# A decoder layer on one core: the first quarter of the dilated heads' projection as seven products instead of eight

## The chip, the core and the metric

The kernel runs on one core of a Trainium2 chip. The metric is the time of one execution in device microseconds, taken as the median of several runs. The core has a matrix engine (PE, or TensorE; its weight loads are shown apart as PEld), a vector engine (DVE), a scalar engine (ACT), a general engine (POOL, or GpSimd), and SyncE (SP), which here only issues transfers. Each engine works through its own list of instructions in order. Semaphores hold an engine back until another has got as far as it must.

## The reference, cut to what matters

The layer has 256 tokens and a width of 2048. All is float32.

```
proj   = rms_norm(x) @ w_in                 # queries, keys, values of 8 + 8 heads, and two gates ga, gb
o_a    = forgetting attention of the 8 fox heads       (256 x 1024)
o_b    = dilated attention of the 8 dilated heads      (256 x 1024)
merged = sigmoid(ga) * (o_a @ w_br_fox) + sigmoid(gb) * (o_b @ w_br_dil)
x      = x + merged @ w_out
x      = x + causal conv-SwiGLU feed-forward of rms_norm(x)
```

The change is in `o_b @ w_br_dil`, a product of 256x1024 by 1024x2048.

## The kernel before, in words

Every large product is cut in units. A unit is one weight tile of two K tiles by 512 columns (128x1024 numbers, 512 KB). SP loads it into one of four raw buffers (`raw`). ACT copies it to a rounded high part (`w_hi`, `high(n)`, line 1480), DVE subtracts that and keeps the rest as the low part (`w_lo`, `low(n)`, line 2086), and PE multiplies three times: high by high, high by low, low by high. Both parts lie in a ring of six (`RING = 6`). So `high(n + 6)` and `low(n + 6)` follow unit n on PE (semaphore `used`), and PE starts unit n when `lo_done` has reached it.

`rows_unit` (lines 874 to 878) is the usual unit: two K tiles, both blocks of 128 tokens, three matmuls each, which makes twelve matmuls of 128x128 by 128x512. A product unit, as `gate_product` or `out_product` issue them, has one block of 128 tokens only, which may be a sum of blocks, against a weight tile that may be a sum of tiles. It has six matmuls. A 2x2 block product needs eight of them plainly and seven by Strassen's and Winograd's scheme. The gates, the output projection and the feed-forward use that scheme already.

The branch stage is 32 row units: 16 for the fox heads (c = 0 to 3 column chunks of 512, u = 0 to 3 pairs of K tiles) and then 16 for the dilated heads. The fox chunks carry the last four softmax heads (12 to 15) between their units: scores after u = 0 (`attend_scores`), transposes of the probabilities after u = 3 (`attend_transpose`), the product with the values after the next chunk's first unit (`last_values`). After each chunk DVE multiplies the two banks by the gates (`fox_part`, `dil_part`). After each dilated chunk it adds both branches into `tmp`, and PE transposes the sum by eight small matmuls (`transpose_block`, line 925) after u = 2 of the next chunk; ACT and DVE split it for the output projection (`merged_high`, `merged_low`).

What sets the order is written out by hand: each engine's loop goes over the units and has its extra work at named units. SP issues branch loads four ahead: load m waits for `lo_done` of load m - 4, which used the same raw buffer. Between them, at m = 14, 17, 20 and 23 (`PAIR_LOADS_AT`), it issues the first four loads of the output projection's own seven-product pair, into `raw_y` and `raw_x`. POOL prepares the bias of softmax heads 13, 14 and 15 (`prepare_dil`, lines 2788 and 2790), each after the row maximum of the head before, and then issues the adding transfers of the output pair (`third_sum`, `first_sum`, line 2814). An adding transfer reads a tile from HBM and adds it to what lies in SBUF; it goes through POOL's software queue.

Of the kernel before, what the change touches and what calls it, by code (L numbers as in the profile page):

```python
# [6 lines left out]
P = 128  # L7
SEQ = 256
# [101 lines left out]
OUT_UNIT = BR_UNIT + 4 * UPR  # L110
# [22 lines left out]
FF_UNIT = OUT_UNIT + len(OUTS)  # L133
GATE_PARTS = ("P3", "P5", "P6")


def raw_use(n):

    if n < GATE_UNIT:
        return n % RAW_SLOTS, n // RAW_SLOTS + 1  # L140
    if n < BR_UNIT:
        k = GATE_LOAD_AT[GATES[n - GATE_UNIT]]
    elif n < OUT_UNIT:
        k = n - BR_UNIT + len(GATE_LOADS)
    else:
        k = OUT_LOAD_AT[OUTS[n - OUT_UNIT]] + 4 * UPR + len(GATE_LOADS)
    return k % RAW_SLOTS, (GATE_UNIT + k) // RAW_SLOTS + 1

# [41 lines left out]
def br_banks(m):  # L190
    return (0, 2) if m % 2 else (1, 3)
# [7 lines left out]
PAIR_LOADS_AT = {14: (1, 0), 17: (1, 1), 20: (0, 0), 23: (0, 1)}  # L199
# [9 lines left out]
TAIL_MADE = {"P5": 13, "P6": 14, "P7": 15, "P3": 16}  # L209
# [60 lines left out]
FIRST_SLOTS = (8, 9, 0, 1, 2, 3)  # L270
# [29 lines left out]
def load_count(k):  # L300

    before = raw_use(FF_UNIT - 1)[1] if slot_of(k) < RAW_SLOTS else 0
    return before + sum(slot_of(m) == slot_of(k) for m in range(k + 1))
# [34 lines left out]
def decoder_layer(nc, x, x_t, smalls, consts, w_in, w_fox, w_dil, w_out, w_up, w_down, decay_dram, out):  # L338
# [15 lines left out]
    with ctx:  # L354
# [116 lines left out]

        def last_of(name, k):
# [70 lines left out]
        def last_sum(m):  # L543
# [25 lines left out]
        xt_in = [sem(f"xt_in{u}") for u in range(UPR)]  # L569
        smalls_in, consts_in, wf_in, x_again, out_done = (  # L570
            sem("smalls_in"), sem("consts_in"), sem("wf_in"), sem("x_again"), sem("out_done"))
        second_tile, third_tile = sem("second_tile"), sem("third_tile")
        first_tile, gains_in, tile_high, tile_split, warm_data = (
            sem("first_tile"), sem("gains_in"), sem("tile_high"), sem("tile_split"), sem("warm_data"))
# [38 lines left out]
        d_seeded = sem("d_seeded")  # L613
        row_max, den_ready, rden_ready, dil_merged, tap1, ss_ready, fa_sum, fa_neg = (
            sem("row_max"), sem("den_ready"), sem("rden_ready"), sem("dil_merged"), sem("tap1"),
            sem("ss_ready"), sem("fa_sum"), sem("fa_neg"))
        decay_rows = [sem(f"decay_rows{m}") for m in range(4)]
# [8 lines left out]
        def _(sp):  # L626
# [11 lines left out]
            def load_late(n, src):  # L638

                if n >= BR_UNIT + RAW_SLOTS:  # L640
                    sp.wait_ge(lo_done, n - RAW_SLOTS)
                s = raw_use(n)[0]
                sp.dma_start(raw[:, s, :].rearrange("p (k n) -> p k n", k=KU), src).then_inc(w_loaded[s], 16)

            def br_tile(m):
                c, u = m // 4 % 4, m % 4
                return (w_fox_v if m < 16 else w_dil_v)[:, KU * u:KU * u + KU, NB * c:NB * c + NB]
# [91 lines left out]
            for n, unit in enumerate(GATES, GATE_UNIT):  # L739
                if unit[0] != "H":  # L740
                    k = GATE_LOAD_AT[unit] + RAW_SLOTS
                    sp.wait_ge(lo_done, n)
                    if k < len(GATE_LOADS):
                        load_gate(k)
                    else:
                        m = k - len(GATE_LOADS)
                        load_late(BR_UNIT + m, br_tile(m))
                    continue
# [10 lines left out]
            for m in range(RAW_SLOTS, 4 * UPR):  # L759
                load_late(BR_UNIT + m, br_tile(m))  # L760
                if m in PAIR_LOADS_AT:
                    side, q = PAIR_LOADS_AT[m]
                    if side:
                        sp.wait_ge(lo_done, GATE_AT["H", PAIRS - 1, "P4", q])
                        load_gate_b22(PAIRS, q)
                    else:
                        sp.wait_ge(y_added[q], 2 * PAIRS)
                        load_gate_b11(PAIRS, q)
# [95 lines left out]
        def _(pe):  # L864
# [273 lines left out]
            def branch_unit(m, u):  # L1138
                pair = [bank[b] for b in br_banks(m)]
                kt = KU * u if m < 4 else KT // 2 + KU * u  # L1140
                rows_unit(BR_UNIT + 4 * m + u, actB, (kt, kt + 1), pair, u == 0, u == 3)
# [23 lines left out]
            for c in range(4):  # L1165
                if c < 2:
                    pe.wait_ge(fox_merged, 3 + c)
                else:
                    pe.wait_ge(dil_merged, c - 1)
                for u in range(4):  # L1170
                    if c == 0 and u == 1:
                        pe.wait_ge(kept_lo, 1)
                    elif c == 0 and u > 1:
                        pe.wait_ge(o_lo, 12 + 2 * (u - 1))
                    branch_unit(4 + c, u)
                    if c == 0 and u == 0:
                        last_values(3)
                    if c and u == 2:
                        pe.wait_ge(merged, c)
                        transpose_block(lambda r, col: tmp[:, r, col:col + P], bank[4:6], mt_ready)  # L1180
# [7 lines left out]
            def out_product(n, name, q):  # L1188

                if q == 0:  # L1190
                    if name == "P3":
                        pe.wait_ge(dil_merged, 3)
                        pe.wait_ge(h_part_lo, 5)
                    elif name == "P1":
                        pe.wait_ge(dil_merged, 4)
                        pe.wait_ge(h_part_hi, 9)
                    elif name == "P7":
                        pe.wait_ge(h_part_lo, 6)
                    elif name == "P6":
                        pe.wait_ge(h_part_lo, 7)  # L1200
                        pe.wait_ge(g_p1, PAIRS + 1)
                    elif name == "P5":
                        pe.wait_ge(h_part_lo, 8)
# [36 lines left out]
            for n, unit in enumerate(OUTS, OUT_UNIT):  # L1240
# [6 lines left out]
                else:  # L1247
                    u = unit[1]
                    if u == 0:
                        pe.wait_ge(g_c22, PAIRS)  # L1250
# [98 lines left out]
            def tail_product(n, name):  # L1349
# [11 lines left out]
                if name in TAIL_PARTS:  # L1361
                    pe.wait_ge(h_part_lo, 8 + TAIL_PARTS.index(name) + 1)
# [60 lines left out]
        def _(act):  # L1423
            def high(n):
# [3 lines left out]
                if pair_product(n):  # L1428
# [14 lines left out]
                    else:  # L1443
                        act.wait_ge(y_added[q], 2 * c + 2)
                elif n < FF_UNIT:
# [328 lines left out]

            for c in range(4):
                for u in range(4):
                    high(BR_UNIT + 4 * c + u + RING)
# [7 lines left out]
                    elif u == 3:  # L1785
                        copy_pt(12 + c)

            for c in range(4):
                for u in range(4):
                    high(BR_UNIT + 16 + 4 * c + u + RING)  # L1790
                    if c == 0 and u == 0:
                        out_high(15)
                    elif c and u == 2:
                        merged_high(c - 1)
                    elif c == 3 and u == 1:
                        act.wait_ge(mt_lo, 2)
                        merged_part_high("P3", 12)
                        for half in range(2):
                            nc.scalar.activation(own[:, 0, :, half * P:half * P + P],
                                                 gate_quarter(0, 0, half).bitcast(f32), ACT.Copy, scale=-1.0)\  # L1800
                                .then_inc(h_part_hi, 1)
# [14 lines left out]
            for n, unit in enumerate(OUTS, OUT_UNIT):  # L1816
# [9 lines left out]
                if unit == ("C", 0):  # L1826
                    merged_part_high("P7", 12)
                elif unit == ("H", PAIRS, "P3", 0):
                    merged_part_high("P6", 12)
                elif unit == ("H", PAIRS, "P3", 1):  # L1830
                    merged_part_high("P5", 12)
# [235 lines left out]
        def _(dve):  # L2067
            def low(n):
# [4 lines left out]
                if pair:  # L2073
                    _, c, name, q = pair
                    src = raw_x[:, q, :] if name in ("P1", "P5", "P2") else raw_y[:, q, :]
                elif n < FF_UNIT:
# [340 lines left out]
            def fox_part(c):  # L2417
                dve.wait_ge(used, BR_UNIT + 4 * c + 4)
# [6 lines left out]
            def dil_part(c):  # L2425
                dve.wait_ge(used, BR_UNIT + 16 + 4 * c + 4)
                for r in range(RT):
                    part = gb[:, r, c * NB:(c + 1) * NB]
                    t = nc.vector.tensor_tensor(part, bank[br_banks(4 + c)[r]], part, ALU.mult)
                t.then_inc(dil_merged, 1)  # L2430
# [3 lines left out]
                                        ALU.add).then_inc(merged, 1)  # L2434

            for c in range(4):
                for u in range(4):
# [5 lines left out]
                    low(BR_UNIT + 4 * c + u + RING)  # L2443
                    if u == 0:
# [3 lines left out]
                        softmax_head(12 + c, prep, True)  # L2448

            def make_merged():  # L2450
# [3 lines left out]
                dve.wait_ge(h_made, 9)  # L2454
                nc.vector.tensor_tensor(x21, x11, x21, ALU.subtract).then_inc(h_made, 1)
                dve.wait_ge(h_made, 10)
                nc.vector.tensor_tensor(x11, x11, x22, ALU.subtract).then_inc(h_made, 1)
                dve.wait_ge(h_made, 11)
# [8 lines left out]
            for c in range(4):  # L2467
                for u in range(4):
                    if u == 3:
                        if c:  # L2470
                            merged_low(c - 1)
                            dve.wait_ge(mt_ready, 2 * c)
                        dil_part(c)
                    low(BR_UNIT + 16 + 4 * c + u + RING)
                    if c == 0 and u == 0:
                        out_low(15)
                    elif c == 3 and u == 0:
                        make_merged()
                    elif c == 3 and u == 2:
                        merged_part_low("P3", 7)  # L2480
# [42 lines left out]
            for n, unit in enumerate(OUTS, OUT_UNIT):  # L2523
# [7 lines left out]
                if unit == ("C", 0):  # L2531
                    merged_part_low("P7", 10)
                elif unit == ("H", PAIRS, "P3", 1):
                    merged_part_low("P6", 11)
                elif unit == ("C", 1):
                    merged_part_low("P5", 12)
# [105 lines left out]
            def tail_low(name):  # L2642

                dve.wait_ge(h_part_hi, 12 + TAIL_PARTS.index(name) + 1)
# [130 lines left out]
        def _(pool):  # L2775
            def prepare_fox(h):
# [3 lines left out]
                pool.wait_ge(decay_rows[h // 2], 32)  # L2780
# [68 lines left out]
            for c in range(1, 4):  # L2849
                prepare_dil(12 + c).then_inc(prep_ready, 1)  # L2850
# [90 lines left out]
```

## Time and profile before

| what | us |
|---|---|
| median of 3 runs | 1331.04 |
| lowest and highest | 1330.64, 1331.25 |
| the profiled execution's own time | 1331.1 |
| its span, first to last instruction | 1329.3 |
| PE busy | 1324.8 |
| DVE busy | 1147.9 |
| ACT busy | 959.9 |
| POOL busy | 167.1 |

The granted TensorE clock was 1.000 over the whole span. The chain of work that ended last lies on PE for 100% of the span. The profile's matmul durations overlap, since matmuls are pipelined: the distance between two starts says more than the duration of one.

### The profile page before, as it was taken

The numbers are of one execution on the slowest core, as the hardware profiler recorded it, in microseconds if no ns is written. First come the engines' busy times: TensorE is split into PE (matmuls) and PEld (weight loads), VectorE is DVE, ScalarE is ACT, GpSimd is POOL, SyncE is SP. The second block draws the span as 40 slices with busy tenths as digits, with TensorE's granted clock in tenths as the row PEclk, the third lists the DMA queues.
The fourth block names the chain that finished last, engine by engine and source line by source line (L and its number), as shares of the span: only waits on it lengthen the run. The fifth ranks groups of instructions, "written<-read, shape, count | busy, mean of one in ns | idle before, by whom it ended". The sixth has DMA issues, their size and how long they took to land.

```text
span 1329.3 us, 16539 instructions
## 1 busy us (share of the span) xinstructions
PE 1324.8 (100%) x6037; PEld 1098.8 (83%) x6037; DVE 1147.9 (86%) x1369; ACT 959.9 (72%) x1214; POOL 167.1 (13%) x186
## 2 busy tenths in 40 slices
PE   9999999999999999999999999999999999999999
PEld 7888888888888888888888888888888888888887
DVE  6868887888878876888689898999999999999998
ACT  6666666566666654567777878888888888888874
POOL 0121212021011000101010101111111102020201
DMA  9877685758888665488879798999989899999996
GB/s 355 290 170 262 142 259 119 244 156 229 230 218 226 219 207 205 129 238 260 288 174 332 161 303 172 314 220 282 248 252 267 230 281 222 294 213 315 192 294 176
DMA packets 120720, 312.03 MB, mean 235 GB/s; under 512 B 12088, under 2 KB 13376, under 8 KB 120384
## 3 DMA queue, kind: packets, MB, share of 16 engines
q1 hardware_dynamic: 92192, 235.10, 50.9%
q0 software_dynamic: 23824, 71.84, 30.4%
q10 hardware_dynamic: 4624, 4.05, 1.0%
q8 instruction: 48, 0.79, 0.2%
q14 instruction: 32, 0.26, 0.1%
HBM read 308.84 MB, written 2.11 MB: 234 GB/s over the span
## 4 chain that ended last, share of the span: by engine, by line
PE 100%; DVE 0%; POOL 0%; issue 0%; POOLq 0%
PE acc L874 12%; PE acc L878 12%; PE acc L876 12%; PE acc L912 9%; PE acc L916 9%; PE acc L914 9%; PE acc L1103 4%; PE acc L1099 4%; PE acc L1101 4%; PE acc L1076 3%; PE acc L1078 3%; PE acc L1074 3%; PE acc L1266 1%; PE acc L897 1%; PE acc L893 1%; PE acc L895 1%
## 5 line engine op out<-in xcount | busy, mean ns | idle before, releaser
L2086 DVE TENSOR_TENSOR w_lo<-raw,w_hi 128x1024 fp32r<-128x1024 f32 x225 | 272.7, 1219 | 67.1 <-ACT w_hi L1480 65.7
L1480 ACT ACTIVATE w_hi<-raw 128x1024 fp32r<-128x1024 f32 x225 | 235.1, 1054 | 86.7 <-PE acc L878 50.2
L874 PE MATMUL acc<-w_hi,actA 128*128 128x512 f32 x580 | 228.3, 394 | 0.0
L878 PE MATMUL acc<-w_hi,actA 128*128 128x512 f32 x580 | 226.1, 390 | 0.0
L876 PE MATMUL acc<-w_lo,actA 128*128 128x512 f32 x580 | 225.8, 389 | 0.0
L1480 ACT ACTIVATE w_hi<-raw_y 128x1024 fp32r<-128x1024 f32 x152 | 158.1, 1058 | 72.9 <-PE acc L878 21.9
L2086 DVE TENSOR_TENSOR w_lo<-raw_y,w_hi 128x1024 fp32r<-128x1024 f32 x152 | 182.8, 1219 | 18.4 <-ACT w_hi L1480 16.8
L2086 DVE TENSOR_TENSOR w_lo<-raw_x,w_hi 128x1024 fp32r<-128x1024 f32 x116 | 139.8, 1220 | 45.4 <-ACT w_hi L1480 45.2
L1480 ACT ACTIVATE w_hi<-raw_x 128x1024 fp32r<-128x1024 f32 x116 | 119.8, 1052 | 47.9 <-DMA raw_x<-w_in 23.0
L878 PEld LDWEIGHTS acc<-w_hi,actA 128*128 128x128 f32 x580 | 108.9, 188 | 22.9
L874 PEld LDWEIGHTS acc<-w_hi,actA 128*128 128x128 f32 x580 | 108.9, 188 | 21.9 <-issue 0.2
L876 PEld LDWEIGHTS acc<-w_lo,actA 128*128 128x128 f32 x580 | 109.0, 188 | 21.8
L912 PE MATMUL acc<-w_hi,actB 128*128 128x512 f32 x296 | 116.3, 393 | 0.0
L916 PE MATMUL acc<-w_hi,actB 128*128 128x512 f32 x296 | 115.4, 390 | 0.0
L914 PE MATMUL acc<-w_lo,actB 128*128 128x512 f32 x296 | 115.1, 389 | 0.0
L1099 PE MATMUL acc<-w_hi,actA 128*128 128x512 f32 x224 | 88.3, 394 | 0.0
L1103 PE MATMUL acc<-w_hi,actA 128*128 128x512 f32 x224 | 87.3, 390 | 0.0
L1101 PE MATMUL acc<-w_lo,actA 128*128 128x512 f32 x224 | 87.2, 389 | 0.0
L1480 ACT ACTIVATE w_hi<-odd 128x1024 fp32r<-128x1024 f32 x64 | 67.5, 1054 | 19.6 <-PE acc L916 9.9
L2086 DVE TENSOR_TENSOR w_lo<-odd,w_hi 128x1024 fp32r<-128x1024 f32 x64 | 77.9, 1217 | 1.8 <-ACT w_hi L1480 1.8
L2857 POOL DMA_DIRECT2D raw_y<-w_up x34 | 29.5, 867 | 376.2 <-DVE w_lo L2086 376.0
L2561 DVE SCALAR_TENSOR_TENSOR work<-acc,smalls_sb,work 128x255 f32<-128x255 f32 (+1 forms) x176 | 72.4, 472 | 3.2 <-ACT work L1863 3.1
(385 smaller groups left out, 2779.5 us busy)
## 6 DMA issues: line engine op xcount, KB each, us to landing
raw<-w_in SPq DMA_DIRECT2D x101, 512.0 KB, 4.8
raw<-w_down SPq DMA_DIRECT2D x59, 512.0 KB, 5.6
raw_x<-w_up SPq DMA_DIRECT2D x44, 512.0 KB, 5.0
raw_y<-w_up POOLq DMA_DIRECT2D x34, 512.0 KB, 7.6
raw_x<-w_in SPq DMA_DIRECT2D x28, 512.0 KB, 4.2
odd<-w_up SPq DMA_DIRECT2D x27, 512.0 KB, 5.1
work<-w_up SPq DMA_DIRECT2D x24, 512.0 KB, 5.5
work<-w_up POOLq DMA_DIRECT2D x24, 512.0 KB, 8.1
```

Of the source, the lines that this page charges most:

```text
L874: nc.tensor.matmul(o, lhsT=a_h, rhs=w_hi[:, s, k, :], start=first and k == 0, stop=False, skip_group_check=onto_seed)
L876: nc.tensor.matmul(o, lhsT=a_h, rhs=w_lo[:, s, k, :], start=False, stop=False, skip_group_check=onto_seed)
L878: mm = nc.tensor.matmul(o, lhsT=a_l, rhs=w_hi[:, s, k, :], start=False, stop=last and k == KU - 1, skip_group_check=onto_seed)
L912: nc.tensor.matmul(o, lhsT=a_h, rhs=w_hi[:, s, k, :], start=first and k == 0, stop=False, skip_group_check=True)
L914: nc.tensor.matmul(o, lhsT=a_h, rhs=w_lo[:, s, k, :], start=False, stop=False, skip_group_check=True)
L916: mm = nc.tensor.matmul(o, lhsT=a_l, rhs=w_hi[:, s, k, :], start=False, stop=last and k == KU - 1, skip_group_check=True)
L1099: nc.tensor.matmul(o, lhsT=a_h, rhs=w_hi[:, s, k, :], start=side == 0 and j == 0 and k == 0, stop=False, skip_group_check=True)
L1101: nc.tensor.matmul(o, lhsT=a_h, rhs=w_lo[:, s, k, :], start=False, stop=False, skip_group_check=True)
L1103: mm = nc.tensor.matmul(o, lhsT=a_l, rhs=w_hi[:, s, k, :], start=False, stop=kt == KT - 1, skip_group_check=True)
L1480: nc.scalar.activation(w_hi[:, n % RING, :, :], src.rearrange("p (k n) -> p k n", k=KU), ACT.Copy).then_inc(hi_done, 1)
L2086: nc.vector.tensor_tensor(w_lo[:, n % RING, :, :], src.rearrange("p (k n) -> p k n", k=KU), w_hi[:, n % RING, :, :].bitcast(f32), ALU.subt ...
L2561: t = nc.vector.scalar_tensor_tensor(out=conv[:, j, lag:SEQ], in0=bank[(4, 7)[j // 2]][:, (j % 2) * SEQ:(j % 2 + 1) * SEQ - lag], scalar=s ...
```

## The change

The dilated chunks 0 and 1 over the first two pairs of K tiles (heads 8 to 11) become one 2x2 block product: two blocks of 128 tokens by two K pairs, times two K pairs by two column chunks. Its eight half units, which were four row units, become seven product units in the order P1, P7, P6, P2, P5, P4, P3. The other twelve units of the dilated heads stay row units; units (0,2), (0,3), (1,2), (1,3) now add onto banks that the products have filled.

- Four blocks of activations are summed: DVE makes four whole blocks (`dil_whole`) and four differences (`make_dil`), ACT rounds them (`dil_high`), DVE takes the low parts (`dil_low`). This is done inside the fox chunks.
- Four of the seven weight tiles are sums. Their first tiles are loaded by SP into `raw_x` and `raw_y` after branch loads 4, 5, 6 and 7 (`load_dil_base`), and POOL adds the others by seven adding transfers (`add_dil_tile`): three for P4, two for P6, one each for P7 and P5. The other three products load one tile each in the ordinary way.
- ACT copies the bank after P1, P7, P6 and P5 (`dil_copy`): P1 negated from bank 1 to bank 3, P5 from bank 1 to bank 0, P7 and P6 into the softmax buffer. PE's P6, P5, P4 and P3 wait for one of these copies each.
- DVE adds the saved P6 to chunk 0's second block, and takes the saved P7 from chunk 1's second block, ahead of the gating.
- The merged chunk 0 is transposed after unit (1,3), and was after (1,2). The merged chunk 1 is added by DVE after unit (2,0).
- The output pair's first loads move to m = 22, 23, 24 and 26 of 31.
- Four semaphores are shared with start-up ones, and counts are shifted. One load fewer in the raw ring turns the first slots of the feed-forward.

```diff
+DIL_STEPS = ("P1", "P7", "P6", "P2", "P5", "P4", "P3")
+DIL_BANKS = {"P1": 1, "P6": 1, "P5": 1, "P7": 7, "P4": 7, "P2": 3, "P3": 0}
+DIL_TILE = {"P1": (0, 0), "P2": (0, 1), "P3": (1, 1)}
+DIL_SUMS = {"P4": (0, ((1, 1), (1, 0), (0, 0), (0, 1))), "P6": (1, ((1, 1), (1, 0), (0, 0))),
+            "P7": (2, ((1, 1), (1, 0))), "P5": (3, ((0, 0), (1, 0)))}
...
-PAIR_LOADS_AT = {14: (1, 0), 17: (1, 1), 20: (0, 0), 23: (0, 1)}
+PAIR_LOADS_AT = {22: (1, 0), 23: (1, 1), 24: (0, 0), 26: (0, 1)}
+DIL_BASE_AT = {4: "P4", 5: "P6", 6: "P7", 7: "P5"}
...
+            def load_dil_base(name):
+                at, tiles = DIL_SUMS[name]
+                q = QU - 1 if name in ("P4", "P6") else 0
+                if name in ("P6", "P7"):
+                    sp.wait_ge(lo_done, GATE_AT["H", PAIRS - 1, "P4", q])
+                else:
+                    sp.wait_ge(y_added[q], 2 * PAIRS)
+                sp.dma_start(dil_at[at].rearrange("p (k n) -> p k n", k=KU), dil_tile(*tiles[0]))\
+                    .then_inc(dil_loaded[name], 16)
...
+            def dil_product(name):
+                if name == "P1":
+                    pe.wait_ge(fox_merged, 3)
+                    pe.wait_ge(h_part_hi, 8)
+                elif name == "P7":
+                    pe.wait_ge(g_c22, PAIRS)
+                elif name == "P6":
+                    pe.wait_ge(dil_out, DIL_OUT["P1"])
+                elif name == "P2":
+                    pe.wait_ge(kept_lo, 1)
+                elif name == "P5":
+                    pe.wait_ge(dil_out, DIL_OUT["P6"])
+                elif name == "P4":
+                    pe.wait_ge(dil_out, DIL_OUT["P7"])
+                elif name == "P3":
+                    pe.wait_ge(dil_out, DIL_OUT["P5"])
...
+            for unit in BRANCH[16:]:
+                if unit[0] == "Q":
+                    dil_product(unit[1])
+                    if unit[1] == "P7":
+                        last_values(3)
+                    continue
...
+            for unit in BRANCH[16:]:            # ACT
+                n = BR_AT[unit]
+                if unit == ("Q", "P7"):
+                    out_high(15)
+                if unit[0] == "Q" and unit[1] in ("P1", "P7", "P6", "P5"):
+                    dil_copy(n, unit[1])
+                high(n + RING)
...
+            add_dil_tile("P4", 1)
+            add_dil_tile("P6", 1)
+            prepare_dil(13).then_inc(prep_ready, 1)
+            add_dil_tile("P7", 1)
+            add_dil_tile("P5", 1)
+            add_dil_tile("P4", 2)
+            prepare_dil(14).then_inc(prep_ready, 1)
+            add_dil_tile("P6", 2)
+            add_dil_tile("P4", 3)
+            prepare_dil(15).then_inc(prep_ready, 1)
```

## Rows read from the trace of the kernel before

**Rows 1.** The page: PE's busy time, and DMA busy tenths in 40 slices.
```profile
PE 1324.8 (100%) x6037; PEld 1098.8 (83%) x6037; DVE 1147.9 (86%) x1369; ACT 959.9 (72%) x1214; POOL 167.1 (13%) x186
...
DMA  9877685758888665488879798999989899999996
```
**Rows 2.** Waits of PE, whole span: waiter, released by, us, times, longest.
```profile
PE acc L999 <- POOL actB L2802: 1.3, 1, 1.3
```
**Rows 3.** The chain that ended last: start, us, what.
```profile
505.79 0.33 PE acc L952 x3
...
525.88 0.87 PE acc L925 x8
537.66 0.87 PE acc L925 x8
```
**Rows 4.** Timeline of PE around the last fox unit and the first dilated one.
```profile
502.91 0.39 PE L874 MATMUL acc<-w_hi,actB 128*128 128x512 f32 x1
...
505.63 0.49 PE L952 MATMUL acc<-smalls_sb,softmax 128*128 128x128 f32 x3
505.88 0.48 PE L874 MATMUL acc<-w_hi,actB 128*128 128x512 f32 x1
...
508.71 0.59 PE L959 MATMUL acc<-softmax,odd 128*128 128x256 f32 x2
...
509.28 0.47 PE L874 MATMUL acc<-w_hi,actB 128*128 128x512 f32 x1
```
**Rows 5.** Timeline of PE in product units of the output projection.
```profile
570.15 0.39 PE L1212 MATMUL acc<-w_hi,actB 128*128 128x512 f32 x1
...
571.51 0.39 PE L1212 MATMUL acc<-w_hi,actB 128*128 128x512 f32 x1
```
**Rows 6.** Timeline of ACT in the branch stage: start, us, instruction, idle before.
```profile
505.89 1.06 ACT L1480 ACTIVATE w_hi<-raw 128x1024 fp32r<-128x1024 f32 x1 [1.66 <-PE acc L878]
506.86 0.47 ACT L1492 ACTIVATE softmax<-acc 128x384 f32<-128x384 f32 x1
...
509.94 0.37 ACT L1500 ACTIVATE actB<-acc 128x256 fp32r<-128x256 f32 x1
...
527.42 0.59 ACT L1509 ACTIVATE actA<-acc 128x512 fp32r<-128x512 f32 x1
```
**Rows 7.** ACT's groups by form, 453 to 610 us: busy us, mean ns.
```profile
L1808 ACT ACTIVATE acc<-acc 128x512 f32<-128x512 f32 x1 | 0.6, 579 | 0.0
```
**Rows 8.** Timeline of DVE: a softmax's end, a gating, and the turn between dilated chunks.
```profile
502.26 0.55 DVE L2125 TENSOR_SCALAR softmax<-softmax,st 128x128 f32<-128x128 f32 x2
...
505.83 1.29 DVE L2422 TENSOR_TENSOR work<-acc,work 128x512 f32<-128x512 f32 x2 [0.35 <-PE acc L878]
...
538.84 1.23 DVE L2086 TENSOR_TENSOR w_lo<-raw,w_hi 128x1024 fp32r<-128x1024 f32 x1 [1.50 <-ACT w_hi L1480]
539.99 1.49 DVE L2137 TENSOR_TENSOR actA<-acc,actA 128x512 fp32r<-128x512 f32 x2
...
542.73 1.23 DVE L2433 TENSOR_TENSOR tmp<-work 128x1024 f32<-128x1024 f32 x1
```
**Rows 9.** The page's DMA queues: packets, MB, share of 16 engines' span.
```profile
q1 hardware_dynamic: 92192, 235.10, 50.9%
q0 software_dynamic: 23824, 71.84, 30.4%
```
**Rows 10.** Engines and DMA share from 449 to 488 us.
```profile
449.00:488.00 39.00, 39.00 (x181) 32.48 (x180) 28.43 (x50) 23.79 (x33) 2.35 (x6) 1.00 0.68 232
```
**Rows 11.** Landing times of raw_x transfers, 380 to 600 us.
```profile
DMA to landing us min/median/max: 3.7/5.4/10.7
```
**Rows 12.** The page's DMA issues: KB, median us to landing.
```profile
raw<-w_in SPq DMA_DIRECT2D x101, 512.0 KB, 4.8
...
raw_y<-w_up POOLq DMA_DIRECT2D x34, 512.0 KB, 7.6
```
**Rows 13.** Timeline of POOL: the preparations for heads 14 and 15.
```profile
475.52 0.18 POOL L2788 COPY st<-smalls_sb 128x1 f32<-128x1 f32 x1 [11.71 <-DVE st L2105]
...
487.58 0.18 POOL L2788 COPY st<-smalls_sb 128x1 f32<-128x1 f32 x1 [10.97 <-DVE st L2105]
```

More of the change, by code:

```diff
@@ L133 @@
 FF_UNIT = OUT_UNIT + len(OUTS)
+OUT_AT_LOADS = [OUT_AT[unit] for unit in OUT_LOADS]
 GATE_PARTS = ("P3", "P5", "P6")
@@ L269 @@
 LOAD_AT = {unit: m for m, unit in enumerate(LOADS)}
[L270 removed]
+FIRST_SLOTS = (8, 9, 3, 0, 1, 2)
 SLOTS = 10
@@ L1786, in _ @@
                         copy_pt(12 + c)
[L1788 to L1801, printed above, removed]
+                    if (c, u) == (1, 1):
+                        act.wait_ge(kept_lo, 1)
+                        dil_high("P1")
+                    elif (c, u) == (2, 1):
+                        for name in DIL_PARTS[:2]:
+                            dil_high(name)
+                    elif (c, u) == (2, 2):
+                        for name in DIL_PARTS[2:]:
+                            dil_high(name)
+            for unit in BRANCH[16:]:
[5 more added lines that the diff above has]
+                high(n + RING)
+                if unit == ("L", 1, 3):
+                    merged_high(0)
+                elif unit in (("L", 2, 2), ("L", 3, 2)):
+                    merged_high(unit[1] - 1)
+                elif unit == ("L", 3, 1):
+                    act.wait_ge(mt_lo, 2)
+                    merged_part_high("P3", 20)
+                    for half in range(2):
+                        nc.scalar.activation(own[:, 0, :, half * P:half * P + P],
+                                             gate_quarter(0, 0, half).bitcast(f32), ACT.Copy, scale=-1.0)\
+                            .then_inc(h_part_hi, 1)
             def out_sum(n, name):
@@ L2465, in merged_part_low @@
                     .then_inc(h_part_lo, 1)
[L2467 to L2480, printed above, removed]
+            for unit in BRANCH[16:]:
+                if unit in (("L", 2, 3), ("L", 3, 3)):
+                    c = unit[1]
+                    merged_low(c - 1)
+                    dve.wait_ge(mt_ready, 2 * c)
+                    dil_gate(c)
+                    merge(c)
+                elif unit == ("L", 0, 3):
+                    dil_gate(0)
+                    merge(0)
+                elif unit == ("L", 1, 3):
+                    dil_gate(1)
+                low(BR_AT[unit] + RING)
+                if unit == ("Q", "P7"):
+                    out_low(15)
+                elif unit == ("L", 2, 0):
+                    merged_low(0)
+                    dve.wait_ge(mt_ready, 2)
+                    merge(1)
+                elif unit == ("L", 3, 0):
+                    make_merged()
+                elif unit == ("L", 3, 2):
+                    merged_part_low("P3", 13)
             def add_x2(n, c, banks):
```

267 lines of the change are left out of this document (201 added, 66 removed).

## The prediction, made before the changed kernel was run

> **What bounds the kernel now.** I read the page's busy times first. PE is busy for 1324.8 us of a span of 1329.3 us; DVE has 1147.9 and ACT 959.9 [rows 1]. That alone doesn't prove a bound, because matmul ends are modelled. So I read PE's waits next: over the whole span there is one, of 1.3 us, before the first matmul [rows 2]. The chain of waits then shows what the branch stage is made of. In it the chain never leaves PE, and two dilated chunks end 11.78 us apart (525.88 to 537.66) [rows 3]. The timeline shows what those 11.78 us are: one row unit of twelve matmuls takes 505.63 - 502.91 = 2.72 us, or 0.227 us per matmul [rows 4], so 48 matmuls take 10.9 us and the eight transposes 0.87. Nothing is left over. In this stage a matmul that goes is worth 0.227 us, and an edit on any other engine is worth nothing until PE has to wait for it.
>
> **What PE loses.** Four row units (48 matmuls) become seven products of six (42). A product unit's pace is not shown in this stage, but the output projection has them: six matmuls from 570.15 to 571.51 take 1.36 us [rows 5], again 0.227 each, so a product costs no start-up of its own. Saved: 6 x 0.227 = 1.36 us. The transposes, the values product and the 0.31 us start behind each of them (505.88 to the next start) stay, in the same number. The Trainium skill, "VectorE: DVE Perf Modes", section "The TRN2 errata", gives a matmul of 512 columns as 518 cycles of 2.4 GHz, 216 ns; by it the sum would be 1.30 us. The rows say 227, and the rest does without it.
>
> **The four new waits of PE on ACT.** I lay the new order over the old clock, from PE's 505.63. Transposes to 505.88; P1 to 507.33 (0.09 us slow start, as the old unit has: 508.71 - 505.88 = 2.83 for twelve); P7 to 508.69; values to 509.28 (0.57 us, 508.71 to 509.28) [rows 4]; P6 to 510.7, P2 to 512.1, P5 to 513.45, P4 to 514.8, P3 to 516.2. ACT starts its part 0.10 us behind PE's last issue (505.89 against the transposes' 505.63, of which 0.16 is the matmul's end) and hands on after 0.97 us for a `high` and 0.5 for a copy of a bank, whose full length is 0.58 to 0.59 [rows 6, 7].
> - P1's copy runs at about 507.6 to 508.2; P6 wants it at 509.28. Free by 1.1 us.
> - Then `high` to 508.9, head 15's output (0.37) after the values, about 509.5 to 509.9, P7's copy to 510.4, a `high` to 511.3, P6's copy to 511.9. P5 wants it at 512.1. Free by 0.2 us only: this is the tightest step, and what is behind it is two more `high`s, which have the ring's lead.
> - P5's copy: two `high`s, then 513.8 to 514.35; P3 wants it at 514.8. Free by 0.4 us. P4's wait for P7's copy is long over.
> A semaphore's way from ACT to PE isn't in a row; the way from PE to ACT is 0.1 to 0.26 us. The bounds of this item are 0 (all three fit) and, at most, three waits of one `high` each, 3 x 0.97 = 2.9 us, if each copy comes one `high` later. I take 0.1 us, since my clock has every copy in time.
>
> **DVE.** It gains three `low`s (3 x 1.22), two bank sums (about 0.65 each, half of 1.29 [rows 8]), eight block sums and four low parts of 128x256, for which I take 0.35 each from half a 128x512 one: 3.7 + 1.3 + 4.2 = 9.2 us over some 110 us in which it has at least 20 us idle. ACT gains three `high`s, four copies and five small roundings, about 7.5 us, and has more room. What matters is place. The block sums sit behind the softmax of their chunk, not before it: a head is finished at 502.8, and PE wants it at 505.63 [rows 4, 8], a slack of 2.8 us that no added DVE work eats. In the seven products DVE must deliver one `low` per 1.36 us of PE; it needs 1.22 plus head 15's low part, but ACT's copies throttle it to about one per 1.3 us. It enters with six units in hand and the first unit behind the products (index 23) is low at about 512.7, wanted at 516.2. Nothing there.
> The transposes of chunk 0 wait for three DVE operations and an addition (0.68 + 2 x 0.6 + 1.22 = 3.1 us), with two units (5.4 us) before them: free. Those of chunk 1 now wait for work moved behind unit (2,0). With T at the last issue of (1,3): transposes and (2,0) to T + 3.6, `high` to T + 4.8, `low` 1.15, low parts of the merged chunk 1.41 (539.99 after 538.84, as now [rows 8]), addition 1.22, in all T + 8.6. PE arrives at T + 0.87 + 2.83 + 2 x 2.72 = T + 9.1. Free by 0.5 us. If that cover goes, each us late is a us of PE. I take 0.
>
> **DMA.** Before, the four units needed four plain transfers. Now it is three plain, four bases and seven adding ones: three plain more and seven adding more. A tile is 0.524 MB, so the page's queues hold 448 plain and 137 adding ones, at 0.509 x 1329.3 / 448 = 1.51 us and 0.304 x 1329.3 / 137 = 2.95 us of all sixteen engines each [rows 9]. Added: 3 x 1.51 + 7 x 2.95 = 25 us. The stretch into which nearly all falls, 449 to 488, is now 68% busy, which is 12.5 us of room in 39 [rows 10]; two output loads leave it. So it fills up and the rest runs on to about 500. The Trainium skill, "DMA: Bandwidth & Descriptors", section "Issuing engines are not separate DMA queues", says that transfers issued by SP and by POOL run on the same 16 engines and interleave. It speaks against this change, and is the mechanism of the first rival; the trace fits it in so far as slices with 9 tenths busy exist all through the feed-forward while PE stays full [rows 1].
> What a late tile costs: a load is issued when its buffer's last user is low, about 2.4 us into an iteration, and is wanted four iterations later: 4 x 2.77 - 2.4 = 8.7 us. Landing takes 4.8 now [rows 12], 10.7 at worst near here [rows 11]. Beyond 8.7 the `high` waits and with it, in ACT's queue, the exponentials of a head; that has 2.8 us of slack, so PE waits from a landing of about 11.5 us. At the other units the ring has 11 us more. The sums themselves have time: bases from about 450, landed by 461; adding ones 7.6 us each [rows 12], of which the last two of P6 and P4 stand in POOL's queue behind head 14's preparation at 475.5 [rows 13], so done at 485 to 487. P6's tile is wanted near 496, P4's at 505.9. POOL's preparations have waited 11 us idle for DVE, so the adds ahead of them (about 1.2 us each to issue) delay none. The item is bounded by 0 and 12 us (four heads, each 3 us late); I take 0, as the nearest row, a 10.7 us maximum, is below the point.
> The moved output loads are issued near 510 to 520 and wanted after 535. Free.
>
> **The sum.** -1.36 + 0.1 = -1.3 us on the profiled execution's 1331.1 us (span 1329.3 and 1.8 around it), so 1329.8. The median shown is 1331.04, 0.06 lower: 1329.8 again. That is 0.10%. About 0.2%, or 2.7 us, is what a measurement of this kernel can tell from no change, so this is "within".
>
> **Rivals.**
> - Late tiles. The stretch from 450 to 500 asks for 22 plain and 7 adding transfers, 34 + 21 = 55 us in 50. If fox tiles behind a base and beside an adding transfer land at 14 us and not at 9, three heads come 2.5 us late each: 7.5 - 1.4 = 6 us slower, 1337. It decides from 11.5 us of landing. For it: the arithmetic above. Against it: the adds are spread in three groups, and the feed-forward lives with 90% busy. 8%.
> - ACT's copies come one `high` late in the seven products: 1 to 3 waits of 0.97 us take the place of the gain, or the 0.5 us before chunk 1's transposes turns negative: 1330.3 to 1332.5. For it: 0.2 us of slack. Against it: every duration is from a row of the same operation. 15%.
> - The change sets something free that the rows don't show, a pace below 0.227 or a shorter end: over 2.7 us faster, 1328 or below. No row speaks for it; PE had no wait to lose. 4%.
> - My forecast, 1329.3 to 1330.3: 73%.
>
> **How the numbers follow.** Faster by over 0.2% is the third rival: 0.04. Slower by over 0.2% is the first: 0.08. The rest, 0.88, is within. The range goes from 1329.2, the full 1.36 and the runs' own spread, up to 1331.7, which takes in most of the second rival, a wait of two `high`s.
>
> **What would show it.** PE from the last fox transposes to the start of unit (0,2): 10.3 us, with products 1.36 apart. A wait of PE on ACT's copy would stand before P5 first, then P3. The transposes (x8) come once after (1,3) and the merged stage ends 1.4 us earlier, and that distance is kept to the last instruction. DMA busy near 0.9 to 1 from 450 to 490, with fox landings up to 9 us. PE waiting for softmax (line 952) or for `lo_done` would prove the first rival. A gain or a loss of over 2.7 us would make the prediction wrong.

## The result: 13 us slower, and the profile after

The changed kernel took 1344.26 us (median of 5 runs, 1341.78 to 1346.02), the kernel before 1331.04 (5 runs, 1330.64 to 1331.43). The ratio is 1.0097, with a 95% interval from 1.0082 to 1.0112. I had forecast 1329.8, within 0.2%. The profiled execution took 1344.27 us, and its span is 1342.5, against 1329.3.

The page of the changed kernel, as [rows 1] before. PE's busy time is up by only 2.7 us, so 10.5 of the 13.2 us by which the span grew are idle time. A row for the clock has appeared, which means that the clock is no longer full everywhere; the mean is 0.996.

```profile
PE 1327.5 (99%) x6031; PEld 1100.1 (82%) x6031; DVE 1156.4 (86%) x1386; ACT 967.4 (72%) x1227; POOL 175.8 (13%) x193
...
PEclk9999999999999989999999999999999999999999
DMA  9877685758888795568869788999999999999996
```

The waits of PE over the whole span, as [rows 2]: two new ones. One is for the copy of head 12's probabilities, the other for the sum of the merged chunk 0.

```profile
PE acc L1024 <- ACT softmax L1608: 6.7, 1, 6.7
PE acc L990 <- DVE tmp L2603: 3.6, 1, 3.6
PE acc L1064 <- POOL actB L3017: 1.3, 1, 1.3
```

The chain that ended last, 440 to 620 us, shows what is behind each (start, us, what). Read it upward from PE. Head 12's values (line 1024) wait for ACT's copy (line 1608). ACT was there late because the `high` ahead of it waited for a fox tile that took 15.0 us from its issue to its landing. That tile was asked for late in turn, since its buffer came free only when a tile that had landed in 8.4 us was split. The second wait is further down: the merged transposes (line 990) wait for DVE's addition (line 2603), and that stands behind the split of a w_dil tile which landed in 10.1 us.

```profile
450.71 8.39 DMA raw<-w_fox
459.12 1.07 ACT w_hi L1596
460.21 1.24 DVE w_lo L2242
461.47 14.98 DMA raw<-w_fox
476.50 0.94 issue
477.44 0.48 ACT softmax L1608
477.96 1.22 PE acc L1024 x2
...
489.45 0.33 PE acc L1017 x3
...
514.67 0.33 PE acc L1017 x3
...
524.14 10.14 DMA raw<-w_dil
534.31 1.07 ACT w_hi L1596
535.44 1.11 issue
536.54 0.68 DVE softmax L2588
...
538.46 1.24 DVE tmp L2603
539.74 1.97 PE acc L990 x8
...
550.54 0.87 PE acc L990 x8
```

The `high` before that one had waited too, for the tile issued at 457.78, which landed only 16.5 us later. So had the last tile alone been in time, the copy could have come at the end of this `high`, 475.4, and not at 477.44: about 2 us of the wait hang on the last tile alone (an estimate from these starts), and the rest on both.

```profile
474.35 1.06 ACT L1596 ACTIVATE w_hi<-raw 128x1024 fp32r<-128x1024 f32 x1 [1.23 <-DMA raw<-w_fox]
```

POOL's issuing of the adding transfers was not what was late. Its preparation of head 13, which stands behind two of them, had waited 3.3 us for DVE:

```profile
465.32 0.18 POOL L3003 COPY st<-smalls_sb 128x1 f32<-128x1 f32 x1 [3.34 <-DVE st L2261]
```

The transfers' share and PE's clock in the stretches around it (us from and to, sum; busy time of PE, PEld, DVE, ACT, POOL; granted clock, DMA share, GB/s), as [rows 10]. Sixteen engines are fully used from 455 to 477. The granted clock shows 0.71 towards the end of PE's 6.7 us of idleness and 0.77 in the stretch behind it, so it stood at 1.2 GHz in part of each and at 2.4 in the rest. From 537 to 547, with the 3.6 us wait in it, it shows 0.83. From 507 to 517 the transfers are nearly idle, and from 527 they are full again.

```profile
449.00:455.00 6.00, 6.00 (x28) 4.97 (x27) 3.96 (x5) 2.55 (x3) 0.00 (x0) 1.00 0.90 292
455.00:461.00 6.00, 6.00 (x29) 5.01 (x28) 3.19 (x4) 2.69 (x3) 1.42 (x2) 1.00 1.00 351
...
473.00:477.00 4.00, 0.00 (x0) 0.00 (x0) 1.56 (x3) 1.71 (x3) 0.78 (x1) 0.71 1.09 298
477.00:487.00 10.00, 9.04 (x34) 7.54 (x35) 6.87 (x18) 6.01 (x13) 2.57 (x4) 0.77 0.99 268
...
507.00:517.00 10.00, 10.00 (x47) 8.25 (x46) 8.73 (x20) 5.01 (x10) 0.00 (x0) 1.00 0.15 52
...
527.00:537.00 10.00, 9.13 (x41) 7.22 (x39) 4.05 (x4) 3.91 (x4) 0.00 (x0) 1.00 1.00 374
537.00:547.00 10.00, 7.26 (x30) 6.25 (x31) 8.56 (x11) 5.24 (x7) 0.00 (x0) 0.83 0.57 179
```

Landing times (from issue to arrival) of the tiles issued from 449 to 480 us: the fox tiles went to 11.1 us in the median, from 4.5 in the kernel before. Over 440 to 540 us the raw tiles' landing times were 3.5, 7.1 and 16.5 us (least, median, most), and in the kernel before 3.5, 4.5 and 6.0.

```profile
raw<-w_fox SPq DMA_DIRECT2D x10, 512.0 KB, 11.1
raw_x<-w_dil POOLq DMA_DIRECT2D x3, 512.0 KB, 9.8
```

The seven products themselves (timeline of PE): from the first product's start to the first row unit behind them, 525.09 - 514.75 = 10.34 us, with no wait.

```profile
514.75 0.48 PE L1240 MATMUL acc<-w_hi,wf 128*128 128x512 f32 x1
...
525.09 0.39 PE L939 MATMUL acc<-w_hi,actB 128*128 128x512 f32 x1
```

**Where the 13 us are.** The same points of PE's program are compared with [rows 3, 4].

| stretch | before | after | difference |
|---|---|---|---|
| up to the fourth fox transposes (x3) | 505.79 | 514.67 | +8.88 |
| from there to the second merged transposes (x8) | 31.87 | 35.87 | +4.00 |
| the rest of the span | 791.6 | 792.0 | +0.3 |

Of the 8.88, 6.7 are waiting and 2.0 slow clock: from head 12's values to the next transposes (x3) it is 489.45 - 477.96 = 11.5 us, and in the kernel before it was 480.58 - 471.06 = 9.5. The 4.00 are the gain of 1.3, the wait of 3.6, and 1.7 of slow clock: the next transposes come 10.80 us later, and 9.10 in a version without the wait (e5 below).

### The profile page after: what moved, and what is told of

It reads as the page before. It is cut to its first block, busy times and chain, and to the rows that moved or that the text cites. A ratio compares the mean times of both kernels' runs of the same rounds, so it can differ in the third digit from the quotient of the medians.

```text
span 1342.5 us, 16579 instructions
## 1 busy us (share of the span) xinstructions
PE 1327.5 (99%) x6031; PEld 1100.1 (82%) x6031; DVE 1156.4 (86%) x1386; ACT 967.4 (72%) x1227; POOL 175.8 (13%) x193
## 4 chain that ended last, share of the span: by engine, by line
PE 96%; DMA 2%; DVE 1%; ACT 0%; issue 0%; POOL 0%; ACTq 0%; POOLq 0%
PE acc L939 11%; PE acc L943 11%; PE acc L941 11%; PE acc L977 9%; PE acc L981 9%; PE acc L979 9%; PE acc L1168 4%; PE acc L1164 4%; PE acc L1166 4%; PE acc L1143 3%; PE acc L1141 3%; PE acc L1139 3%; DMA raw<-w_fox 2%; PE acc L1378 1%; PE acc L958 1%; PE acc L962 1%
## 5 line engine op out<-in xcount | busy, mean ns | idle before, releaser
L1596 ACT ACTIVATE w_hi<-odd 128x1024 fp32r<-128x1024 f32 x64 | 67.4, 1053 | 19.4 <-PE acc L981 10.1
```

Source lines behind the costliest of these rows:

```text
L1596: nc.scalar.activation(w_hi[:, n % RING, :, :], src.rearrange("p (k n) -> p k n", k=KU), ACT.Copy).then_inc(hi_done, 1)
```

## The experiments

Theory A: the adding transfers and bases crowd the fox tiles, a late tile stands in ACT's queue before work that PE needs, and that is the first wait. Theory A2: the output tiles among the w_dil tiles behind the seven products are the second. The rival B: the added work on ACT, DVE and POOL, and its order, is what is late. Rival C: the bases alone, ahead of the fox tiles in SP's queue.

**e1, without the adding transfers.** The seven `add_dil_tile` calls are out, and ACT waits for the base alone.

```diff
-                    act.wait_ge(dil_summed[summed_product(n)], 16 * (len(tiles) - 1))
+                    act.wait_ge(dil_loaded[summed_product(n)], 32)
...
-            add_dil_tile("P4", 1)
-            add_dil_tile("P6", 1)
...
```

> The changed kernel without its seven adding transfers; the four base tiles are still loaded, so four weight tiles are not the sums they should be. Theory A (late tiles: the adding transfers make the fox tiles land late, ACT's queue stands behind them and PE waits 6.7 us for head 12's probabilities): the first wait and its slow clock go, 9 us; the second wait (3.6 us before the transposes of chunk 0, with 1.5 us of slow clock) has another cause and stays: 1335. Rival B (the added ACT and DVE work, or POOL's order, is late): nothing changes, 1344. Rival C (the four bases ahead of the fox tiles in SP's queue do it): nothing changes in the first wait either, 1343 to 1344.

Measured: 1335.58 us against 1331.06, ratio 1.0035 (1.0023 to 1.0047). Its waits:

```profile
PE acc L990 <- DVE tmp L2603: 2.4, 1, 2.4
PE acc L1064 <- POOL actB L3017: 1.3, 1, 1.3
PE acc L1038 <- DVE w_lo L2383: 0.2, 1, 0.2
```

The first wait is gone and the second stays, shorter. The bases alone bring the fox tiles to 6.0 us of landing, which is harmless (against C). All ACT and DVE work was kept (against B). Behind the wait of 2.4 us the eight transposes took 1.39 us and not 0.87, and the next ones came 10.91 us later, against 9.10 in e5: 1.8 us of slow clock, with the granted clock at 0.83 from 527 to 537.

**e2, the old kernel with the new traffic.** It computes as before; the bases and adding transfers are issued at the changed kernel's places, and nothing reads them. Its output loads move to the matching late places, and each waits until the sum in its buffer is complete.

```diff
+DIL_BASE_AT = {4: "P4", 5: "P6", 6: "P7", 7: "P5"}
-PAIR_LOADS_AT = {14: (1, 0), 17: (1, 1), 20: (0, 0), 23: (0, 1)}
+PAIR_LOADS_AT = {23: (1, 0), 24: (1, 1), 25: (0, 0), 27: (0, 1)}
...
+                if m in DIL_BASE_AT:
+                    load_dil_base(DIL_BASE_AT[m])
...
+            add_dil_tile("P4", 1)
+            add_dil_tile("P6", 1)
             prepare_dil(13).then_inc(prep_ready, 1)
...
```

> The kernel before, computing as before, with the changed kernel's four bases and seven adding transfers into raw_x and raw_y at the same places of SP's and POOL's orders (nothing reads the sums), and the output pair's first loads moved to the same late places (m = 23, 24, 25 and 27 of 32). Theory A: the first wait appears in the old kernel, PE waits 6 to 7 us for head 12's values, and with the slow clock it is 9 us slower: 1340. The second wait needs the burst behind the seven products and doesn't appear, or is under 1 us. Rival B: no wait of PE, 1331.

Measured: 1341.14 us, ratio 1.0070 (1.0053 to 1.0087). Its longest wait, and from its chain the transfer at the root of it:

```profile
PE acc L980 <- ACT softmax L1513: 6.9, 1, 6.9
```

```profile
461.54 15.49 DMA raw<-w_fox
```

The old kernel gets the same wait from the traffic alone, and no wait before its merged transposes. This is the cleanest proof of theory A: 10.1 us of loss without any product, copy or block sum. By the trace 9.6 of them are there at the fourth fox transposes (515.42 for 505.79) and 0.5 is lost in the output projection. (I expected 9; another wait, of 0.8 us, is of PE for a head's probabilities themselves, line 973 on DVE.)

**e3, the output pair's loads split.**

```diff
-PAIR_LOADS_AT = {22: (1, 0), 23: (1, 1), 24: (0, 0), 26: (0, 1)}
+PAIR_LOADS_AT = {20: (1, 0), 21: (1, 1), 28: (0, 0), 29: (0, 1)}
```

> The changed kernel with the output pair's first loads at m = 20 and 21 (into raw_y, free once P7 and P6 are split, where the transfers stand nearly idle from 507 to 517 us) and m = 28 and 29 (into raw_x), not at 22, 23, 24 and 26. Theory A2 (these four tiles among five w_dil tiles issued within 8 us make a w_dil tile land in 10 us, and chunk 0's gating stands behind its low part): the second wait goes and its slow clock, 5 us: 1339, the first wait untouched. Rival (the second wait is that of the three w_dil tiles that are issued late because the products free no raw buffer; the output loads don't matter): 1343 to 1344.

Measured: 1338.98 us, ratio 1.0056 (1.0041 to 1.0071), 5.3 us less than the changed kernel. The 6.7 us wait is as it was, and that for line 2603 is gone. Theory A2 holds, and its rival, the late w_dil loads alone, does not: the same five loads are issued from 519.6 to 526.1 us here, and PE doesn't wait. The w_dil tiles issued from 517 to 530 us landed in 5.7 us in the median, for 8.2.

**e4, the bases before the fox tiles and the adds spread.**

```diff
+                elif name == "P2":
+                    load_dil_base(("P5", "P4")[q])
+                elif name == "P4":
+                    load_dil_base(("P7", "P6")[q])
...
             add_dil_tile("P4", 1)
-            add_dil_tile("P6", 1)
             prepare_dil(13).then_inc(prep_ready, 1)
-            add_dil_tile("P7", 1)
-            add_dil_tile("P5", 1)
-            add_dil_tile("P4", 2)
+            add_dil_tile("P6", 1)
             prepare_dil(14).then_inc(prep_ready, 1)
+            add_dil_tile("P7", 1)
+            add_dil_tile("P4", 2)
             add_dil_tile("P6", 2)
+            add_dil_tile("P5", 1)
             add_dil_tile("P4", 3)
```

> The changed kernel with the four bases loaded at the end of the gate stage (where the transfers are 30% busy from 440 to 449 us) and the adding transfers spread: P4's first before head 13's preparation, P6's first before head 14's, the other five between head 14's and head 15's. Output pair loads untouched. Theory A in the form that it is the crowding of 455 to 477 us: the first wait falls from 6.7 to below 1 us, 1336 with the second wait as it was. Rival (too many bytes for the stage, wherever they are): PE waits 3 us or more at another fox chunk, 1340 or above.

Measured: 1338.24 us, ratio 1.0048 (1.0033 to 1.0063). This was a partial miss. The first wait went, but the four bases, now straight in front of the first fox tiles, opened one of 1.9 us inside the first fox chunk. The profile names no releaser for it ("issue"), but ACT had just stood idle for 5.9 us until a fox tile landed, its `high` starting at 455.36 us; that the bases made this tile late is likely and not shown apart. The second wait is the changed kernel's 3.6.

```profile
PE acc L992 <- DVE tmp L2605: 3.6, 1, 3.6
PE acc L941 <- issue: 1.9, 1, 1.9
```

**e5, the compute side alone.** No bases, no adding transfers, the output loads as in e3.

```diff
-                if m in DIL_BASE_AT:
-                    load_dil_base(DIL_BASE_AT[m])
...
-                    act.wait_ge(dil_summed[summed_product(n)], 16 * (len(tiles) - 1))
```

> The changed kernel without the four bases and the seven adding transfers (four weight tiles are then whatever the buffers hold, so the products are not the right ones), and with the output pair's loads split as in e3. All of the seven products, copies, block sums and waits stay. Theory A (transfers are the whole loss, and the compute side of the change works as forecast): both waits are gone, 1331.05 - 1.36 = 1329.7, between 1329.4 and 1330.3. Rival (the copies and the order of ACT and DVE cost something too, hidden so far behind the transfers): 1331 or above.

Measured: 1330.39 us against 1331.13, ratio 0.9995 (0.9986 to 1.0003); 0.1 us beyond the upper end of what I expected, and a gain that this comparison can't tell from none, so the trace has to. Chain:

```profile
505.88 0.33 PE acc L1015 x3
...
527.33 0.90 PE acc L988 x8
536.43 0.87 PE acc L988 x8
```

From the fourth fox transposes to the second merged ones it is 30.55 us, against 31.87 in [rows 3]: 1.32 us gained, where I had forecast 1.36 less 0.1. About 0.5 is lost again by 600 us, where the output projection's transposes come 0.7 earlier than before; this version, like e3 and e7, loads two of its output tiles at m = 28 and 29. The rival expected 1331 or above, and is refuted only as far as the trace goes.

**e7, all seven adds, but later.** Bases untouched, output loads as in e3.

```diff
+            prepare_dil(13).then_inc(prep_ready, 1)
             add_dil_tile("P4", 1)
             add_dil_tile("P6", 1)
-            prepare_dil(13).then_inc(prep_ready, 1)
+            prepare_dil(14).then_inc(prep_ready, 1)
             add_dil_tile("P7", 1)
-            add_dil_tile("P5", 1)
             add_dil_tile("P4", 2)
-            prepare_dil(14).then_inc(prep_ready, 1)
             add_dil_tile("P6", 2)
+            prepare_dil(15).then_inc(prep_ready, 1)
+            add_dil_tile("P5", 1)
             add_dil_tile("P4", 3)
-            prepare_dil(15).then_inc(prep_ready, 1)
```

> The changed kernel with its bases where they are (m = 4 to 7), the output pair's loads as in e3, and the seven adding transfers later: two behind head 13's preparation, three behind head 14's, two behind head 15's. Theory A with the crowding of 455 to 477 us as the cause: the wait of 6.7 us goes; if the stage has room for the adds behind it, 1330 to 1331. Theory A with too many bytes for the stage: the stretch from 475 to 505 us is full (5 adds, 15 us, with the fox and dilated tiles in 30 us) and PE waits 1 to 5 us for a later head or for P4's or P5's tile: 1332 to 1336.

Measured: 1332.20 us against 1331.13, ratio 1.0007 (0.9998 to 1.0016). The wait of 6.7 us is 1.4 now:

```profile
PE acc L1024 <- ACT softmax L1608: 1.4, 1, 1.4
```

So 12 of the 13 us come back with the same bytes, only the order changed. Two orders changed, though: e3 has the same output loads and is 7.9 us above its kernel before, e7 1.1, so 6.8 of the 12 are the adds' and the rest the output loads'. What differs in the first 28 us is not the transfers' share, but the number of adds in it, two for five, and the fox tiles' landing, 7.1 us in the median for 11.1. The stretch behind takes the other adds, 93% busy, and PE doesn't wait in it. Where the adds stand moves these late tiles; by how much each single add does was not tried. Windows of e7:

```profile
449.00:477.00 28.00, 26.62 (x122) 21.90 (x121) 19.47 (x33) 17.48 (x21) 3.39 (x4) 1.00 1.00 313
477.00:507.00 30.00, 30.00 (x142) 24.94 (x142) 24.85 (x57) 16.32 (x33) 7.99 (x9) 1.00 0.93 238
```

**e9, the bases later as well** (m = 8, 9, 10 and 12; output loads at 20, 21, 25 and 26).

```diff
-DIL_BASE_AT = {4: "P4", 5: "P6", 6: "P7", 7: "P5"}
+DIL_BASE_AT = {8: "P4", 9: "P6", 10: "P7", 12: "P5"}
```

> As e7 (all seven adding transfers), with the bases at m = 8, 9, 10 and 12 instead of 4 to 7 and the output pair's raw_x loads at m = 25 and 26 instead of 28 and 29. The 1.4 us wait of e7, which the bases among the first fox tiles cause, goes, and 0.5 us in the output projection: 1330.3 (1329.8 to 1331). Rival (the bases then crowd the adds of 475 to 500 us and a later head is late): 1332 to 1334.

Measured: 1331.06 us against 1331.28, ratio 1.0000 (0.9991 to 1.0009). Better than e7 in the median, but both theories were half right. PE is busy for all of 449 to 477, so e7's wait for the first head is gone; two shorter ones have come behind it, in a stretch that is now 98% busy; that this is their cause is argued, not shown. A third, of 0.8 us, lies in the output projection. The execution profiled here was the slowest of the eleven, 1332.56 us. The waits of PE and that window:

```profile
PE acc L1064 <- POOL actB L3017: 1.3, 1, 1.3
PE acc L1024 <- ACT softmax L1608: 0.9, 2, 0.7
PE acc L1344 <- ACT odd L1966: 0.8, 1, 0.8
```

```profile
477.00:507.00 30.00, 29.06 (x135) 23.59 (x134) 23.84 (x55) 15.73 (x30) 7.35 (x8) 1.00 0.98 270
```

**e6, fewer transfers.** P6's tile is P7's plus P1's, and P4's is P6's plus P2's. DVE makes both additions from tiles that lie in SBUF anyway. The buffers and semaphores that change with it are left out of this cut.

```diff
+                if unit in (("Q", "P7"), ("Q", "P2")):
+                    other = BR_AT["Q", "P1"] if unit[1] == "P7" else n
+                    dve.wait_ge(lo_done, n)
+                    nc.vector.tensor_tensor(dil_at[0], dil_at[0], raw[:, raw_use(other)[0], :],
+                                            ALU.add).then_inc(dil_added, 1)
...
+DIL_BASE_AT = {7: "P7", 10: "P5"}
+PAIR_LOADS_AT = {14: ((1, 1),), 20: ((0, 1),), 21: ((0, 0), (1, 0))}
...
+            prepare_dil(13).then_inc(prep_ready, 1)
+            add_dil_tile("P7", 1)
+            prepare_dil(14).then_inc(prep_ready, 1)
+            add_dil_tile("P5", 1)
+            prepare_dil(15).then_inc(prep_ready, 1)
```

> Seven products with the sums made otherwise: two bases and two adding transfers (P7's and P5's tiles); P6's and P4's tiles come from P7's by two DVE additions of 128x1024 (1.22 us each) of the tiles that P1 and P2 load anyway. Bases at m = 7 and 10, the adds behind the preparations of heads 13 and 14. The two raw_x and raw_y buffers that are now free take output tiles at m = 14 and 20, the other two at m = 21. Added against the kernel before: 1 plain and 2 adding transfers, 1.5 + 2 x 2.95 = 7 us of the transfers' time in place of 25. Theory A: no fox tile lands beyond 9 us, no wait of PE: 1329.7 (1329.4 to 1330.5). Rival (any adding transfer beside the fox stage makes tiles late): PE waits 2 us or more for a softmax head or a gating, 1332 or above.

Measured: 1331.21 us against 1331.13, ratio 1.0000 (0.9991 to 1.0010). One of the eleven executions took 2724.7 us, for which I have no cause; the others lay between 1329.96 and 1331.93. A miss: no fox tile was late (7.0 us at most), but the merged transposes waited.

```profile
PE acc L1068 <- POOL actB L3030: 1.3, 1, 1.3
PE acc L994 <- DVE tmp L2616: 0.8, 1, 0.8
PE acc L1039 <- ACT actA L1708: 0.4, 1, 0.4
```

**e8, e6 with two output loads later.**

```diff
-PAIR_LOADS_AT = {14: ((1, 1),), 20: ((0, 1),), 21: ((0, 0), (1, 0))}
+PAIR_LOADS_AT = {14: ((1, 1),), 20: ((0, 1),), 25: ((1, 0),), 26: ((0, 0),)}
```

> As e6, with the last two of the output pair's first loads at m = 25 and 26 instead of both at m = 21. In e6 PE waited 0.8 us for chunk 0's addition because w_dil tiles landed beside these two loads; with them later the wait goes and the whole 1.2 us that e5 showed up to the last chunk is kept to the end: 1330.0 (1329.6 to 1330.4). Rival (the wait is the DVE's own load, which is busy for the whole stretch 527 to 537): no change from e6, 1331.2.

Measured: 1330.24 us against 1331.28, ratio 0.9992 (0.9983 to 1.0001), span 1328.4 against 1329.3. The wait for DVE's `tmp` is gone:

```profile
PE acc L1068 <- POOL actB L3030: 1.3, 1, 1.3
PE acc L1042 <- DVE w_lo L2396: 0.2, 1, 0.2
```

The rival, that DVE's own load makes the wait, is refuted. This is the fastest version that computes the layer, 1.0 us under the kernel before and about 14 us under the changed one. Its interval still takes in 1, so as a gain over the kernel before it is not clear of the noise.

## Why the prediction was wrong, by its own steps

- **What bounds the kernel**: right. Of the 13.2 us of span all but about 0.5 are waits of PE or its clock behind a wait, less the 1.3 gained.
- **What PE loses, 1.36 us**: right. Forecast from the first product to the first row unit 10.3 us, measured 10.34; e5 shows 1.32 gained by the second merged transposes.
- **The four waits on ACT's copies**: right as to the result. PE waited for none of the four in any version's trace.
- **DVE**: right in the changed kernel, in that its own work delayed nothing. The wait for its addition came from what stood in front of it. In e6 the same place was 0.8 us short again and, with other tile times, free (e8).
- **DMA, the step that failed.** Its first half held: the queues' shares after give 2.9 us per adding transfer and 1.5 per plain one, as I had reckoned. I also wrote that the stretch fills up, and that "I take 0, as the nearest row, a 10.7 us maximum, is below the point". That was wrong in three ways. The 10.7 was the most of a few raw_x transfers, was not near this stretch (it fell between 580 and 600 us, with the engines 81% busy), and says nothing of a full one; there the fox tiles took 11.1 us in the median and up to 16.5. I took the adds as "spread in three groups" over 450 to 500, but five of the seven and all four bases fell in the first 28 us, in which the kernel before had 35% of 28, 10 us, of room for what asks for 4 x 1.5 + 5 x 2.9 = 20. And I gave a tile 8.7 us from its issue, but its issue is itself behind the landing of the tile before in the same buffer: 8.4 and then 15.0 us in series. The first landing, although below my point, took the slack of the second. The bases were late as well, up to 15.0 us, and the adds took 9.5 to 9.8 in the median and not 7.6, but PE waited for no sum.
- **The victim** was not the one named: not the exponentials, but the copy of the probabilities (line 1608). It stands behind the `high` of the chunk's last unit, and PE wants it 2.8 us after the transposes. The ring's eleven us in hand cover splits, not this copy, so they take nothing off the wait.
- **"The moved output loads ... Free", the second step that failed.** I checked when these four tiles are wanted, not whom they delay. The products need only three raw buffers for seven units, so the next w_dil loads are issued late and then within a few us, after a stretch in which the transfers were 15% busy. Five of them and the four output tiles make 9 x 1.5 = 14 us of transfers asked for in 8. A w_dil tile lands in 10.1 us, and DVE's gating and addition of chunk 0, behind its low part, come 3.6 us after PE wants them. e3 takes this away by moving the four loads. I had also put PE's slow clock behind a wait at nothing, since the forecast had no wait: it cost 2.0 and 1.7 us.
- **The rival of late tiles**, at 8% and 1337, had the mechanism and the sign. It took three heads 2.5 us late each, where one copy came 6.7 us late, and it lacked the second wait and PE's slow clock behind both. Its sum has a slip: 22 plain transfers at 1.51 us are 33 us, not 34, so it asks for 54 us in 50; nothing hangs on it. The Trainium skill, "DMA: Bandwidth & Descriptors", section "Issuing engines are not separate DMA queues", says that transfers of all issuing engines run on the same 16 DMA engines and interleave. e2 agrees: with POOL's adding transfers and the bases beside them SP's fox tiles landed in 10.8 us in the median, for 4.5.

What stays open: why e5 loses 0.5 us in the output projection. Its two late output tiles are not the whole answer. From the fourth merged transposes to those near 600 us it takes 39.54 us, and 39.00 in the kernel before; but e8, whose last two output tiles are loaded earlier, at m = 25 and 26, takes 39.40, and e1, with the changed kernel's loads, 39.36, where the changed kernel itself takes 39.04.

## What to carry to other kernels

A transfer that is added is to be priced not by its own engine time against the mean room of a stage, but by how late it makes the others in the few us where it is issued; ask which loads follow one another in one buffer, and what stands behind the waiting split in the in-order queues. Of the same bytes five adds in 28 us cost 9 us here and two cost 1.4: the place of the adds decided, and the busy share (1.03 and 1.00) didn't show it. Where the products took fewer raw buffers, the loads behind them bunched, and other loads in that moment cost 5 us, so look for such a moment and keep it free. Making sums from tiles that lie in SBUF anyway gave the fastest version (e8, 1330.2, against 1331.1 with all seven adds in e9), by less than these comparisons tell apart.

## What the runs showed of the hardware

- Under a full load of adding and plain transfers a plain tile of 512 KB landed in 11.1 us in the median and up to 16.5, instead of 4.5, although each kind's time on the engines (2.9 and 1.5 us, from the shares of the whole span) was unchanged. At the same share of the engines, but two adds for five, it was 7.1 (e7).
- Behind a wait of 3.6 us PE ran its next work slowly: eight transposes took 1.97 us instead of 0.87, and the unit behind them began slowly too, 1.7 us in all. Behind the 6.7 us wait it was 2.0 us, and behind e1's 2.4 us wait 1.8. Behind the waits of 1.9 us in e4 and 0.7 to 1.4 in e7, e6 and e9 the granted clock stayed at 1.00.
